# Turning gathered expert rows on VectorE instead of TensorE, in a fused attention, retention and expert layer

## What is computed

```python
h2 = rms_norm(x, norm2_g)                         # (512, 1024)
# per token: the best of 4 groups, then the best 2 of its 4 experts, weights w
for e in range(16):
    y = (silu(h2 @ w_gate[e]) * (h2 @ w_up[e])) @ w_down[e]   # 1024 -> 512 -> 1024
    out = out + combine[:, e:e+1] * y             # zero for tokens that did not pick e
return rms_norm(x + out, final_norm_g)
```

## Time and profile before

| | |
|---|---|
| median of three runs | 558.14 us |
| the profiled execution | 557.73 us, span of its trace 556.1 us |
| TensorE busy | 537.3 us, 97% of the span |
| VectorE busy | 422.5 us, 76% |
| ScalarE busy | 354.6 us, 64% |
| GpSimd busy | 125.9 us, 23% |
| granted TensorE clock | 0.999 of full speed |
| moved by DMA | 144.03 MB, mean 259 GB/s |

### The profile page before, as it was taken

How to read it: one execution, slowest core, us unless ns; L and a number is a source line. 1 busy time by engine, 2 the same in 40 slices (tenths; PEclk the granted TensorE clock), 3 DMA queues, 4 the chain that set the end, 5 groups by cost and what they waited for, 6 DMA issues and landing times.

```text
span 556.1 us, 7878 instructions
## 1 busy us (share of the span) xinstructions
PE 537.3 (97%) x2669; PEld 435.2 (78%) x2670; DVE 422.5 (76%) x577; ACT 354.6 (64%) x472; POOL 125.9 (23%) x113
## 2 busy tenths in 40 slices
PE   3999999999999999999999999999999999999995
PEld 3988777777877888877788888888888888888883
DVE  2563599564864753488988889888988899888986
ACT  4573654770326163355777887887887887887745
POOL 2360000000000000031343234423343234410520
PEclk9999999999999999999999999999999999999999
DMA  8999222323020236639999999999999999999696
GB/s 286 374 277 394 70 75 77 75 77 76 1 77 0 77 113 244 237 138 313 348 384 388 372 370 363 395 373 368 372 379 385 375 371 370 380 375 398 193 209 212
DMA packets 63772, 144.03 MB, mean 259 GB/s; under 512 B 3784, under 2 KB 13312, under 8 KB 63616
## 3 DMA queue, kind: packets, MB, share of 16 engines
q1 hardware_dynamic: 56624, 120.77, 61.2%
q0 software_dynamic: 7120, 22.90, 13.7%
HBM read 132.77 MB, written 14.30 MB: 264 GB/s over the span
## 4 chain that ended last, share of the span: by engine, by line
PE 83%; DMA 7%; DVE 4%; issue 2%; ACT 2%; POOL 1%; POOLq 0%; DVEq 0%
PE ps L1478 23%; PE ps L1480 22%; PE ps L1479 22%; PE ps L1485 7%; DMA res<-y_dram 4%; PE ps L1628 2%; PE ps L1614 2%; DMA y_dram<-y,row_info 1%; PE ps L1590 1%; PE ps L1560 1%; DMA arena<-norm_g 1%; PE ps L1655 1%; DMA arena<-h_dram,meta 1%; PE ps L1498 1%; DVE act_lo L1004 1%
## 5 line engine op out<-in xcount | busy, mean ns | idle before, releaser
L1289 DVE TENSOR_TENSOR lo_ring<-arena,hi_ring 128x2048 fp32r<-128x2048 f32 x94 | 215.2, 2290 | 28.1 <-ACT hi_ring L878 27.1
L1478 PE MATMUL ps<-hi_ring,act_hi 128*128 128x512 f32 x576 | 232.4, 403 | 0.8 <-DVE act_lo L1004 0.6
L1480 PE MATMUL ps<-hi_ring,act_lo 128*128 128x512 f32 x576 | 225.2, 391 | 0.0
L1479 PE MATMUL ps<-lo_ring,act_hi 128*128 128x512 f32 x576 | 224.6, 390 | 0.0
L878 ACT ACTIVATE hi_ring<-arena 128x2048 fp32r<-128x2048 f32 x94 | 180.2, 1917 | 19.1 <-PE ps L1480 19.1
L1478 PEld LDWEIGHTS ps<-hi_ring,act_hi 128*128 128x128 f32 x576 | 108.3, 188 | 26.5 <-issue 5.0
L1480 PEld LDWEIGHTS ps<-hi_ring,act_lo 128*128 128x128 f32 x576 | 108.1, 188 | 23.5
L1479 PEld LDWEIGHTS ps<-lo_ring,act_hi 128*128 128x128 f32 x576 | 108.5, 188 | 20.1
L994 DVE SCALAR_TENSOR_TENSOR lo_ring<-arena,over,hi_ring 128x512 fp32r<-128x512 f32 x40 | 29.3, 747 | 29.6 <-ACT hi_ring L697 29.5
L600 POOL DMA_INDIRECT y_dram<-y,row_info x14 | 13.2, 945 | 133.6 <-issue 133.6
L1004 DVE TENSOR_TENSOR act_lo<-ps,act_hi 128x512 fp32r<-128x512 f32 x56 | 36.7, 683 | 7.1 <-ACT act_hi L727 5.9
(11 more groups left out here) (235 smaller groups left out, 531.1 us busy)
## 6 DMA issues: line engine op xcount, KB each, us to landing
arena<-w_gate SPq DMA_DIRECT2D x32, 1024.0 KB, 16.7
arena<-w_up SPq DMA_DIRECT2D x32, 1024.0 KB, 17.9
arena<-w_down SPq DMA_DIRECT2D x32, 1024.0 KB, 16.2
arena<-w_in SPq DMA_DIRECT2D x16, 512.0 KB, 8.2
y_dram<-arena POOLq DMA_DIRECT2D x8, 512.0 KB, 11.5
res<-y_dram POOLq DMA_DIRECT2D x8, 512.0 KB, 9.7
arena<-w_in SPq DMA_DIRECT2D x3, 1024.0 KB, 12.9
res<-x SPq DMA_DIRECT2D x4, 512.0 KB, 8.3
```

The lines of the kernel that those rows point to most:

```text
L1289: nc.vector.tensor_tensor(lo(N1 + n12), raw(n12), hi(N1 + n12).bitcast(F32), ALU.subtract).then_inc(lo_done, 1)
L1478: nc.tensor.matmul(dst, a_hi, b_hi, start=start, stop=False)
L1479: nc.tensor.matmul(dst, a_hi, b_lo, start=False, stop=False)
L1480: return nc.tensor.matmul(dst, a_lo, b_hi, start=False, stop=stop)
```

## The change

Rows of h2 are fetched as quarter pieces of 256 values. Piece j of the buffer holds, on partition group q, the q-th quarter of the row of list slot 32j + (partition within the group). So one VectorE transpose in blocks of 32x32 gives the turned rows for all 128 partitions, in `x_raw`, with partition p holding values 8p to 8p+7 of each token. Gate and up weights are loaded to match: partition p takes rows 8p to 8p+7, in runs of 8 KB. TensorE's eight transposes a step go (except for expert 0), ScalarE and VectorE take the rows from `x_raw` in SBUF, in one instruction each. `x_raw` is the memory of `gain2`, so the load of the final gain moves behind the last expert. The piece lists of all experts are made once, by 16 small matmuls and one VectorE instruction. The length of a list no longer cuts its gather: each gather is four indirect DMAs of 128 partitions.

```diff
+        x_pieces = [v.rearrange("p (j f k) -> p k j f", j=QUADS, k=KD) for v in x_rows]
+        x_cols = x_rows[0].rearrange("s (p k) -> s k p", k=KD)
+        x_raw = gain2
...
-        w_gate_v = w_gate.rearrange("a e (k p) n -> (a e) p k n", p=P)
-        w_up_v = w_up.rearrange("a e (k p) n -> (a e) p k n", p=P)
+        w_gate_v = w_gate.rearrange("a e (p h k) n -> (a e) p h (k n)", h=2, p=P)
+        w_up_v = w_up.rearrange("a e (p h k) n -> (a e) p h (k n)", h=2, p=P)
...
# GpSimd, start
-            for b in range(2):
-                pool.indirect_dma_start(x_rows[b], None, h2_dram, bass.IndirectOffsetOnAxis(ap=meta[:, 4 * b:4 * b + 1], axis=0),
-                                        bounds_check=last_token, oob_is_err=False).then_inc(rows_in[b], 16)
-            pool.dma_start(gain2, bass.AP(final_g.tensor, 0, [[0, P], [1, D]])).then_inc(gain_in, 16)
+            pool.indirect_dma_start(x_rows[0], None, h2_dram, bass.IndirectOffsetOnAxis(ap=meta[:, 0:1], axis=0),
+                                    bounds_check=last_token, oob_is_err=False).then_inc(rows_in[0], 16)
+            def gather_pieces(b, idx):
+                for j in range(QUADS):
+                    pool.indirect_dma_start(x_rows[b][:, j * PIECE:(j + 1) * PIECE], None, h2_pieces,
+                                            bass.IndirectOffsetOnAxis(ap=idx[:, j:j + 1], axis=0),
+                                            bounds_check=last_piece, oob_is_err=False).then_inc(rows_in[b], 16)
+            pool.wait_ge(quads_ready, 1)
+            gather_pieces(1, piece_idx[:, QUADS:2 * QUADS])
# GpSimd, every step
-                nc.gpsimd.tensor_copy(gather_idx[:, b:b + 1], meta[:, bass.ds(e * 4, 1)]).then_inc(idx_ready, 1)
+                idx = gather_idx[:, QUADS * b:QUADS * b + QUADS]
+                nc.gpsimd.tensor_copy(idx, piece_idx[:, bass.ds(e * QUADS, QUADS)]).then_inc(idx_ready, 1)
                 pool.wait_ge(idx_ready, e - 1)
                 pool.sem_inc(pool_passed, 1)
-                by_length(e, lambda n: pool.indirect_dma_start(
-                    x_rows[b][0:n, :], None, h2_dram, bass.IndirectOffsetOnAxis(ap=gather_idx[0:n, b:b + 1], axis=0),
-                    bounds_check=last_token, oob_is_err=False).then_inc(rows_in[b], 16))
+                gather_pieces(b, idx)
...
-                    pool.wait_ge(x_turned, e * 2 + 4)
-                    pool.wait_ge(rows_in[1 - b], e * 8 + (16 + 8 * b))
+                    pool.wait_ge(rows_turned, e + 1)
+                    pool.wait_ge(rows_in[1 - b], e * 32 + (64 - 16 * b))
# GpSimd, behind the last step
+            pool.wait_ge(x_lo, E + 1)
+            pool.dma_start(gain2, bass.AP(final_g.tensor, 0, [[0, P], [1, D]])).then_inc(gain_in, 16)
# ScalarE
+            def rows_hi(b, e):
+                act.wait_ge(rows_turned, e)
+                nc.scalar.activation(act_hi[:, b * D:(b + 1) * D], x_raw, ACT.Copy).then_inc(x_hi, 1)
             def step(b, e, q, first=False, last_two=False):
+                if not first or b:
+                    act.wait_ge(mm_done, e * PER_E + (used_value(N1 + 3) - PER_E))
+                rows_hi(1 - b, e + 1)
                 for c in range(PER_E):
                     split(n + c, n12, q * 16 + 16 * (1 + (4 + PER_E * b + c) // RING2))
-                    if c == 0:
-                        (two copies of the turned rows out of PSUM)
# VectorE
+            def rows_lo(b, e):
+                dve.wait_ge(x_hi, e + 2)
+                nc.vector.tensor_tensor(act_lo[:, b * D:(b + 1) * D], x_raw, act_hi[:, b * D:(b + 1) * D].bitcast(F32),
+                                        ALU.subtract).then_inc(x_lo, 1)
+            def turn_rows(b, wait):
+                dve.wait_ge(rows_in[b], wait)
+                nc.vector.transpose(x_raw.rearrange("p (k j r) -> p k j r", k=KD, j=QUADS), x_pieces[b]
+                                    ).then_inc(rows_turned, 1)
...
-            def step(b, e):
+            def step(b, e, last=False):
+                rows_lo(1 - b, e + 1)
                 for c in range(PER_E):
                     split(e * PER_E + 4 + c, (4 + PER_E * b + c) % RING2)
-                    if c == 0:
-                        rows_lo(1 - b, e * 2 + 3)
+                    if c == 3 and not last:
+                        turn_rows(b, e * 32 + (80 + 16 * b))
...
+            turn_rows(1, 16 * QUADS)
             split(3, 3)
# TensorE
-            keep_clock(21, 0)
+            pe.wait_ge(list_copied, 1)
+            for j in range(QUADS):
+                own = slice(j * QUARTER, (j + 1) * QUARTER)
+                for q in range(QUADS):
+                    ins = nc.tensor.matmul(ps[q * QUARTER:(q + 1) * QUARTER, 6, j * E:(j + 1) * E], ident[:, own], list_f,
+                                           start=True, stop=True)
+            ins.then_inc(quads_made, 1)
+            keep_clock(6, 0)
...
                 product(1, xt[b], 0, *at(0), True, False)
-                turn_rows(1 - b, e * 8 + (16 + 8 * b), e * 2 + 2)
                 product(1, xt[b], 4, *at(1), False, True)
-                pe.wait_ge(x_lo, e * 2 + 4)
+                pe.wait_ge(x_lo, e + 3)
```

More of the change, by code:

```diff
@@ L51 @@
 UNITS = (S // P - 1) * E
-QUARTER = P // 4
+QUADS = 4
+QUARTER = P // QUADS
+PIECE = D // QUADS
 START_FILL = (2, 4, 5)
@@ L310, in build @@
         x_turned, x_hi, x_lo = sem("x_turned"), sem("x_hi"), sem("x_lo")
+        rows_turned, list_copied, quads_made, quads_ready, base_set = (
+            sem(n) for n in ("rows_turned", "list_copied", "quads_made", "quads_ready", "base_set"))
         silu_ready, hid_ready, hid_turned, hid_hi, hid_lo = (
@@ L444, in load_expert @@
                 else:
-                    sp.dma_start(as_chunks(raw(slot)), w[kind][e][:, 4 * half:4 * half + 4, :]).then_inc(w2_in[slot], 16)
+                    sp.dma_start(raw(slot), w[kind][e][:, half, :]).then_inc(w2_in[slot], 16)
             def kind_of(s):
@@ L484, in load_unit @@
                     for i, w in enumerate((w_gate_v, w_up_v)):
-                        sp.dma_start(as_chunks(raw(2 * i + half)), w[bass.ds(e, 1), :, 4 * half:4 * half + 4, :]
-                                     .rearrange("e p k n -> (e p) k n")).then_inc(ov_w, 16)
+                        sp.dma_start(raw(2 * i + half), w[bass.ds(e, 1), :, half, :]
+                                     .rearrange("e p n -> (e p) n")).then_inc(ov_w, 16)
                     sp.dma_start(as_chunks(raw(4 + half), 2 * SEG), w_down_v[bass.ds(e, 1), :, 2 * half:2 * half + 2, :]
@@ L891, in step @@
                     split(n + c, n12, q * 16 + 16 * (1 + (4 + PER_E * b + c) // RING2))
-                    if c == 0:
-                        for a in range(2):
-                            act.wait_ge(x_turned, e * 2 + 3 + a)
-                            nc.scalar.activation(xt[1 - b][0][:, 4 * a:4 * a + 4, :],
-                                                 ps[:, 4 + a, :].rearrange("p (k s) -> p k s", k=4),
-                                                 ACT.Copy).then_inc(x_hi, 1)
                     if c == 2:
@@ L1290, in split, with first_rows_lo @@
                                         ALU.subtract).then_inc(lo_done, 1)
[L1293 removed]
+            def first_rows_lo():
                 for a in range(2):
[L1295 removed]
+                    row_lo(xt[0][1][:, 4 * a:4 * a + 4, :], 4 + a, xt[0][0][:, 4 * a:4 * a + 4, :], x_hi, 1 + a, x_lo)
+            def rows_lo(b, e):
[6 more added lines that the diff above has]
+                                    ).then_inc(rows_turned, 1)
             find_ranks(0, EARLY, ps[:, 1, 0:EARLY * E])
@@ L1381, in _ @@
                     step(b, q * 2 + b)
-            step(0, E - 2)
+            step(0, E - 2, last=True)
             dve.wait_ge(silu_ready, E)
@@ L1836, in _ @@
             for a in range(2):
-                turn(4 + a, [x_rows[0][:, (4 * a + i) * P:(4 * a + i + 1) * P] for i in range(4)]).then_inc(x_turned, 1)
+                turn(4 + a, [x_cols[:, 4 * a + i, :] for i in range(4)]).then_inc(x_turned, 1)
             pe.wait_ge(weights_set, 2)
@@ L1855, in multiply_unit @@
                 for a in range(2):
-                    ins = turn(4 + a, [x_rows[0][:, (4 * a + i) * P:(4 * a + i + 1) * P] for i in range(4)])
+                    ins = turn(4 + a, [x_cols[:, 4 * a + i, :] for i in range(4)])
                 ins.then_inc(ov_pe, 1)
```

34 lines of the change are left out of this document (18 added, 16 removed).

## The result

The changed kernel takes 585.29 us, the median of five runs (583.58 to 596.61), against 556.95 for the kernel before (five runs, the three of above among them, 556.13 to 559.97): ratio 1.051, 95% interval 1.047 to 1.054. It is slower by 28.3 us. The run of 596.61 was a slow one and does not count in the ratio. The profiled execution took 590.15 us, its span is 588.4.

A forecast was written before the change was run, and what follows sets the result against it. TensorE was taken to pace the 17.93 us step, with GpSimd deciding after the change. 557.7 + 3.3 (steps) + 0.8 (start) + 1.3 (end) = 563.1 us, 563.5 against the median; range for 8 in 10: 550 to 578.

The forecast's parts named there:

- GpSimd's loop, 18.15 us: Expert step: scatter, index copy, four gathers, `row_info`, two scalings take 18.15 us against 17.93; taken as +0.25 over 13 steps, 3.3.
- Case A: Whole kernel, the likeliest case: the terms as summed, 563.5 us, own range 559 to 568; chance 0.44.
- The fourth gather in the gap of the transpose: GpSimd in the expert step: fourth gather issued at 14.5 us, beside VectorE's transpose, done at 15.5.
- case B: Same GpSimd loop, fourth gather issued just after the fifth split began: step 20.3 us, total 587 to 591; chance 0.12.
- Waits for the end of a running two-input subtraction, then takes 0.93: GpSimd instructions reading SBUF: each waits out VectorE's running subtraction, then takes 0.93 us (a DMA) or 0.13 (a copy).
- The transpose at 1.2 us: VectorE in the expert step: the added transpose of 1024 elements was taken to cost 1.2 us, with 2.4 possible.
- Rival D: VectorE: strided transpose takes 2.4 us, so VectorE needs 18.1, with waits 18.3 to 19.2; total 565 to 577; chance 0.12.
- ScalarE's chain, 5.95 us and a best step of 17.5: Behind the last down product: scaling, rows copy, rounding, lo part take 5.95 us; TensorE stalls 0.4, best step 17.5.
- VectorE's sum of 16.9: VectorE's work per expert step with the transpose at 1.2 us: 16.9 us, just inside 17.5; with 2.4 it is 18.1.
- Start, 0.8: Start of the expert stage: transpose and rows' copy make the product starting at 265.90 come some 0.8 us later.
- End, 1.3: Kernel end: final gain's load on GpSimd ahead of the accumulating DMAs, 0.6 and 0 to 1.3 more; taken as 1.3 us.
- Rival C: Faster: GpSimd's row copy stays ahead of ScalarE's scaling; step 17.5, total 554.6 us, or 17.06 and 549; chance 0.32.

The follow-up runs named there:

- one_gather: Changed kernel with one gather of 128 whole rows instead of four of pieces, `row_info` copy still last, rows in wrong order: 561.38 us, ratio 1.0082.
- perm_info: `info_first` with h2 stored in permuted order by the second norm, so the transpose reads dense and results are right: 554.3 us, ratio 0.9968.
- dense_turn: Changed kernel with the VectorE transpose reading its input without stride, values in wrong order, same instructions: 584.11 us, ratio 1.0457.
- info_first: Changed kernel with GpSimd's `row_info` copy moved ahead of the four gathers instead of behind them: 563.72 us, ratio 1.0119.
- early_rows: `perm_info` with ScalarE's rounding of the rows moved ahead of the scaling, one expert earlier: 550.74 us, ratio 0.9903.

## Why the prediction was wrong

The direction, the engine and the wait that costs the time (ScalarE's scaling behind four gathers and `row_info`) were right; the size was not, 563.5 against 585.3, and outside the range.

- **The step that failed: GpSimd's loop, 18.15 us, and in it "scatter issued at 1.8, past the subtraction at 2.2, done 3.1".** Counted from the end of the scaling as there, the scatter of 400.18 is issued at 1.7 and done at 8.7. The four gathers then end at 12.6, 14.8, 16.1 and 21.3 instead of 8.2, 11.1, 14.2 and 15.5, and `row_info` at 21.5 instead of 16.8. The scatter was held like this in five of the fourteen whole steps, each time with a scaling 3.8 to 4.9 us late, and behind each late scaling TensorE ran at the lower clock for a while, which no term of the sum has. The fourteen steps average 19.98 us. The term of +0.25 over 13 steps, 3.3 us, is 28.7 us.
- **Case A's figure came up by chance.** Four steps take 18.07 to 18.15 us, but not as the loop has it: in them `row_info` is ready 1.5 us or more ahead of the scaling (377.32 for 378.82), which waits for TensorE. It is VectorE's work that sets them: 18.04 to 18.15 in `one_gather` with the transpose of 2.17 us, 17.57 in `perm_info` with that of 1.24.
- **"The fourth gather in the gap of the transpose"** was what hung on 0.05 us. `dense_turn` has the transpose of 1.2 us that I assumed, and there case B's loop runs, within 0.1 us at each gather: in the step shown the fourth gather is issued at 376.62, 0.11 us after the fifth subtraction has begun (376.51), and waits it out; the step is 20.3. The whole takes 584.11, near B's 587. With the price that I took for the transpose, B was the right case, and it had 0.12. A loop where one gather's fortune rests on 0.05 us should have had B as likely as A. That the changed kernel, with the other price and by another way, takes nearly the same time as `dense_turn` is a coincidence as far as these runs show.
- **"Waits for the end of a running two-input subtraction, then takes 0.93"** was true of most and not of all. The 0.93 holds nearly (0.80 to 0.94 from the end of the instruction that let it in). But an instruction may miss the end of one and be held through two to five two-input instructions: two at 336.84 (4.86 us), four at 400.18 (7.0), five in `info_first` (10.36 to 10.41). The held scatters make the steps of 21.2 us, and with a held gather on top those of 22.3. The rows of before showed VectorE back to back hardly anywhere around a GpSimd instruction, so this could not be seen in them; one case (246.36) was taken as proof that one always gets in.
- **The transpose at 1.2 us** is 2.166. Rival D's price of 2.4 was near and its rule held: the Trainium skill (SBUF — State Buffer, section "Door 1: The DMA port swizzle") has float32 free only up to a stride of four, and by the rows it is 2.17 us with a stride of 32 bytes and 1.24 dense. Alone it did not set the time: `dense_turn`, without the stride, was 1.2 us shorter, within the spread of its runs (580.16 to 586.49). But once the copy is out of the way it is the bound: 18.07 in `info_first`, 17.57 in `perm_info`. So D's 18.3 was about right as a step, in a kernel whose `row_info` is in time.
- **ScalarE's chain, 5.95 us and a best step of 17.5**: 5.82 and 17.57 in `perm_info`. Right. **VectorE's sum of 16.9**: 16.8 busy per step of 17.17 in `early_rows` (195.3 of 200). Right, at the dense price.
- **8 KB runs buy nothing**: right, 0.9993. **Start, 0.8**: 1.2. **End, 1.3**: 2.4 in the changed kernel, but for another reason. With the same gain load `info_first` is 0.3 us shorter than before behind the last product silu times up; in the changed kernel the last scatter (543.19) was held for 6.58 us, and the accumulating DMAs follow it.
- **Rival C** (faster, 17.5 or 17.06): the steps exist, but need `row_info` early and a dense read. The four gathers did not take the 1.5 us less that it needs.

The sum is now, by medians: 28.3 us, of which the late `row_info`, with the lower clock behind it, 21.6 (585.3 to 563.7). The other 6.8, in the trace of `info_first`: the eleven steps of 18.04 to 18.14 instead of 17.93 make 1.7; three steps in which the transpose waits for a piece that GpSimd was held with (18.52, 18.73, 20.94) make 4.4; the last short one 0.6; the start 1.2 and the end -0.3. That is 7.6, the span's difference of 7.7.

## What to carry to other kernels

Before adding instructions to an engine that is idle most of the time, look at what is queued behind them and who waits for that. Here one copy of 0.2 us, moved ahead of four gathers, took back three quarters of the loss, and with a dense read and ScalarE's rounding moved the same change gained 1%. On GpSimd count not the instruction's own time alone, but up to a whole two-input VectorE instruction (2.2 us here) on top for each one that touches SBUF, and where VectorE runs back to back, allow for several. If a loop closes with a margin of 0.05 us, forecast both ways of it with equal weight.

## What the runs showed of the hardware

**GpSimd can be passed over several times.** The timeline of the changed kernel has gathers that were issued 0.46 to 0.49 us after the first of two back-to-back subtractions began, and between these two a scatter:

```profile
295.53 4.46 DVE L1315 TENSOR_TENSOR lo_ring<-arena,hi_ring 128x2048 fp32r<-128x2048 f32 x2
296.02 2.65 POOL L590 DMA_INDIRECT arena<-h_dram,gather_idx  x1 [0.30 <-issue]
...
400.18 7.00 POOL L623 DMA_INDIRECT y_dram<-y,row_info  x1 [4.78 <-issue]
...
414.47 4.44 DVE L1315 TENSOR_TENSOR lo_ring<-arena,hi_ring 128x2048 fp32r<-128x2048 f32 x2
414.93 4.86 POOL L590 DMA_INDIRECT arena<-h_dram,gather_idx  x1 [0.30 <-issue]
```

The first got in after one subtraction, as did one at 498.60 (2.64 us); the other only after two (4.86). The scatter at 400.18 was held for 7.0 us, through the end of a subtraction, that for the rows, two lo parts and up to the product silu times up, which has one input in PSUM. VectorE's own instructions were not slower for it (L1315: 2.28 us on average, 2.29 before). What decides who gets in was not found. It is not the moment of the issue alone, as far as the trace resolves it: gathers issued 0.49 us after the start of such a pair passed after one subtraction (296.02) or were held for 10.41 us (350.64 in `info_first`), and scatters issued about 0.6 us before an end passed in 1.44 us (364.03) or were held for 6.96 (322.16). Indirect DMAs of over 4 us stand only in the expert steps of the changed kernel, `info_first` and `one_gather`, whose VectorE has a strided transpose and next to no gap; in `dense_turn`, `perm_info` and `early_rows` the longest takes 3.1 us.

The Trainium skill (SBUF — State Buffer, section "SBUF: two separate sides") has the two engines share a port pair as an exclusive lock, the loser blocked while the other's instruction runs. The waits of up to 3 us agree. That a waiting instruction may be passed over at the next boundary too, for up to 10.41 us, is what these rows add.

**An instruction with one SBUF input lets GpSimd through.** Gathers beside the transpose take 1.00 us (335.54), though it reads and writes 1024 elements per partition for 2.17 us.

**A block transpose of 128x1024 float32** takes 1.24 us read dense, about as long as a subtraction of that size with two inputs (1.22), and 2.17 read with a stride of 32 bytes.
